# In the attention core, VectorE masks item w before it normalises item w-1

## What is computed

```
def attend_block(qb, keys, values, masks, sink):
    scale = HEAD_DIM ** -0.5
    ...
        s = jnp.einsum('bqkgd,bskd->bkgqs', qb, kp).astype(jnp.float32) * scale
        if mk is not None:
            s = jnp.where(mk, s, NEG_INF)
    ...
        m = jnp.maximum(m, jnp.max(s, axis=-1))
    denom = jnp.exp(sink_f - m)
    ...
        p = jnp.exp(s - m[..., None])
        denom = denom + jnp.sum(p, axis=-1)
        out = out + jnp.einsum('bkgqs,bskd->bqkgd', p.astype(vp.dtype), vp).astype(jnp.float32)
    out = out / jnp.moveaxis(denom, -1, 1)[..., None]
```

## Time and profile before

| | |
|---|---|
| time, median of 3 runs | 2988.97 us (2988.23 to 2990.68) |
| profiled execution, first to last instruction | 2988.2 us |
| profiled execution's own time | no more than 0.1 us from the fastest run, so nothing to speak of lies around the span |
| TensorE busy | 2801.6 us (94%) |
| VectorE busy | 1607.8 us (54%) |
| ScalarE busy | 1184.5 us (40%) |
| chain of work that ended last | TensorE 86%, VectorE 6%, ScalarE 6% |
| attention cores | 187.6 to 343.0 us and 2287 to 2442.7 us |

### The profile page before, as it was taken

How to read it: one execution, slowest core, us unless ns; L and a number is a source line. 1 busy time by engine, 2 the same in 40 slices (tenths; PEclk the granted TensorE clock), 3 DMA queues, 4 the chain that set the end, 5 groups by cost and what they waited for, 6 DMA issues and landing times.

```text
span 2988.2 us, 51513 instructions
## 1 busy us (share of the span) xinstructions
PE 2801.6 (94%) x19936; PEld 2645.5 (89%) x19936; DVE 1607.8 (54%) x2878; ACT 1184.5 (40%) x2042; POOL 109.7 (4%) x71
## 2 busy tenths in 40 slices
PE   5977799999998999999989999999998779999999
PEld 4965699999998999999969999999997569999999
DVE  2667556625644664366342665366367754663662
ACT  2347445414423552243232543244234754541441
POOL 1000010000002000000201000000100001000000
PEclk7989899999999999999989999999998989999999
DMA  6410133323320332333201332333121002221222
GB/s 233 181 64 1 50 125 134 137 74 135 136 93 33 138 134 103 123 133 130 66 24 57 120 134 100 111 134 127 63 78 36 1 15 61 78 84 64 73 85 74
DMA packets 62431, 279.67 MB, mean 94 GB/s; under 512 B 7392, under 2 KB 9568, under 8 KB 49632
## 3 DMA queue, kind: packets, MB, share of 16 engines
q1 hardware_dynamic: 62304, 277.93, 27.0%
HBM read 274.74 MB, written 3.16 MB: 93 GB/s over the span
## 4 chain that ended last, share of the span: by engine, by line
PE 86%; DVE 6%; ACT 6%; issue 2%; DMA 1%; SPq 0%; POOL 0%; DVEq 0%; ACTq 0%
PE ps L457 73%; ACT prob L923 3%; PE ps L541 3%; PE ps L480 3%; PE ps L743 1%; PE ps L552 1%; DVE prob L1265 1%; DVE prob L1282 1%; PE ps L502 1%; DMA ada_w<-in_ada_w 1%; ACT stat L925 1%; PE ps L680 1%; PE ps L649 1%; PE ps L510 1%; PE ps L635 1%
## 5 line engine op out<-in xcount | busy, mean ns | idle before, releaser
L457 PE MATMUL ps<-h_hi,w_hi 128*128 128x322 f32 x3392 | 799.8, 317 | 7.2 <-DVE w_lo L1057 4.1
L457 PE MATMUL ps<-h_lo,w_hi 128*128 128x322 f32 x3392 | 784.8, 313 | 0.0
L457 PE MATMUL ps<-h_hi,w_lo 128*128 128x322 f32 x3392 | 780.6, 312 | 0.0
L803 ACT ACTIVATE w_hi<-w_raw 128x1024 fp32r<-128x1024 f32 (+1 forms) x288 | 325.5, 1130 | 1037.1 <-PE ps L457 921.1
L457 PEld LDWEIGHTS ps<-h_hi,w_hi 128*128 128x128 f32 x3392 | 569.6, 190 | 34.0 <-issue 28.4
L457 PEld LDWEIGHTS ps<-h_lo,w_hi 128*128 128x128 f32 x3392 | 577.4, 190 | 0.0
L457 PEld LDWEIGHTS ps<-h_hi,w_lo 128*128 128x128 f32 x3392 | 577.0, 190 | 0.0
L1057 DVE TENSOR_TENSOR w_lo<-w_raw,w_hi 128x1024 fp32r<-128x1024 f32 (+1 forms) x288 | 377.3, 1310 | 67.6 <-ACT w_hi L803 65.9
L1177 DVE SCALAR_TENSOR_TENSOR x<-ps,mods,x 128x321 f32<-128x321 f32 (+5 forms) x264 | 99.9, 435 | 537.1 <-PE ps L457 537.1
L457 PE MATMUL ps<-f_hi,w_hi 128*128 128x322 f32 x1408 | 325.1, 312 | 0.0
L457 PE MATMUL ps<-f_hi,w_lo 128*128 128x322 f32 x1408 | 324.5, 312 | 0.0
(11 more groups left out here) (119 smaller groups left out, 2533.1 us busy)
## 6 DMA issues: line engine op xcount, KB each, us to landing
ada_w<-in_ada_w SPq DMA_DIRECT2D x96, 1024.0 KB, 5.5
w_raw<-in_w_in SPq DMA_DIRECT2D x176, 512.0 KB, 3.6
w_raw<-in_w_out SPq DMA_DIRECT2D x64, 704.0 KB, 4.0
w_raw<-in_w_qkv SPq DMA_DIRECT2D x24, 512.0 KB, 5.1
w_raw<-in_w_o SPq DMA_DIRECT2D x16, 512.0 KB, 3.8
w_raw<-in_w_fnet SPq DMA_DIRECT2D x8, 512.0 KB, 3.6
x<-in_x SPq DMA_DIRECT2D x1, 2576.0 KB, 15.5
out_y<-x SPq DMA_DIRECT2D x8, 322.0 KB, 3.7
```

Source lines behind the costliest of these rows:

```text
L457: mm = pe.matmul(ps[:, 2 * par + hf, 0:NH], w[par][:, kk, :], b[:, hf * NH:(hf + 1) * NH], start=(kk == 0 and n == 0), stop=(kk == k - 1 a ...
L803: act.activation(w_hi[par][:, 0:k, :], w_raw[par][:, 0:k, :], ACT.Copy).then_inc(hi_made, 1)
```

## The change

In VectorE's list `masked(w)` and `normed(w-1)` change places, in all 40 items of both attention layers. All functions, waits and semaphores stay as they are, and so do the lists of the other engines.

```diff
                     for w in range(w0, w0 + 43):
+                        if w < w0 + 40:
+                            masked(w)
                         if 1 <= w - w0 <= 40:
                             normed(w - 1)
-                        if w < w0 + 40:
-                            masked(w)
                         if w - w0 >= 3:
                             out_lo(w - 3)
```

## The result

| | before | changed |
|---|---|---|
| time, median | 2989.16 us (2988.23 to 2990.68) | 3052.47 us (3048.67 to 3055.38) |
| span of the profiled execution | 2988.2 us | 3053.6 us |
| VectorE busy, ScalarE busy | 1607.8, 1184.5 us | 1606.7, 1195.0 us |
| from the first L1279 to the last, first and second core | 146.0, 145.5 us | 175.2, 178.6 us |

Each time is the median of four runs. The profiled run of the changed kernel was the slowest of its four, 3055.38 us, so differences between profiles come out some 3 us larger than those between medians.

A forecast was written before the change was run, and what follows sets the result against it. A ring of waits through ScalarE was taken to bound both attention cores; the swap puts in TensorE's transposes and scores. 2988.2 + 2 x (20 ring + 17 clock) + 0.8 = 3063 us, chance 0.58; range 3020 to 3091.

The forecast's parts named there:

- What bounds the core: Both attention cores: no engine full; normalisation, masking and ScalarE's exponentials form a ring of waits, 4.10 us a turn.
- TensorE's leg: TensorE's transposes and the scores queued behind them, covered before the swap; 1.03 + 1.14 us in blocks 1 and 2.
- What enters the ring: In each core, masking now waits for transposes, then scores on TensorE; ScalarE's exponentials leave the ring.
- The turns: Time per item at full clock: 4.88 us in blocks 1 and 2, 4.44 in block 3, 4.10 in block 0.
- the hand-over from TensorE to VectorE: From the end of the scores to the masking, blocks 1 and 2: 0.05 us, bounds 0 and 0.1.
- The ring's sum: Longer turns over all blocks, clock as before: 20 us a core, 40 us for both.
- The clock: TensorE's clock falls in each core; a third of 31 turns at half level, 1.6 us each: 17 us a core.
- rival A: Both cores: the ring lengthens and the clock stays as before; 3029 us, chance 0.24.
- B: Rival: the clock stays at half level throughout the core, 50 us a core; 3129 us, chance 0.06.
- D: Rival: no change, as the leg is near 1.1 us or VectorE's steps keep the old rhythm; chance 0.06.
- C: Rival: the swap gains, exponentials hidden, VectorE's own 3.2 us an item is the ring; 2919 us, chance 0.06.

The follow-up runs named there:

- e4: Kernel before the change (normalisation first) with TensorE's scores one item further ahead; 2988.83 us.
- e10: Kernel before the change (normalisation first) with scores one item further ahead and a third pair of prob buffers; 2989.18 us.
- e12: Kernel before the change with TensorE doing the second head's transposes of each item twice; 2989.12 us.
- e1: Changed kernel with TensorE's list alone altered, scores one item further ahead; 2960.88 us.
- e3: Changed kernel with scores one item further ahead and a third pair of prob buffers; 2915.95 us.
- e2: Changed kernel with a third pair of prob buffers, TensorE's list as it was; 3049.21 us.
- e5: Changed kernel with TensorE computing each item's values twice into the same place; 3036.01 us.
- e7: Kernel before the change with each head's score matmuls issued twice; 3019.61 us.

## Why the prediction was right, step by step

- **What bounds the core** (a ring through ScalarE, TensorE's leg covered by 0.87 us): shown by e4, e10 and e12, in which TensorE's leg is shortened, freed or lengthened by 0.44 us in the old order and nothing moves.
- **What enters the ring** (transposes, then scores): shown by e1 to e3. Of the two waits the queue is the outer one, as e2 shows, and the buffer the next, as e1 shows.
- **The turns.** Forecast 4.88, 4.44 and 4.10 us, measured 4.95, 4.59 and 4.19. Four terms of block 1 are right within 0.01 (1.72, 0.94, 1.03, 1.14 against 1.72, 0.93, 1.02, 1.15). The mis-sized one is the hand-over from TensorE to VectorE: 0.05, taken from a hand-over to ScalarE, and outside its upper bound of 0.1; it is 0.13. The two engines do not hand over more slowly: in e1 VectorE's masking starts 0.04 behind TensorE (241.68 to 241.72), as ScalarE did, and its turn is 0.93 + 1.09 + 0.04 + 1.72 = 3.78 us. `masked(w)` waits for two semaphores. The masking instruction itself carries the wait for `t_done`, the last one in e1. The wait for `s_done`, the last one in the changed kernel, is an instruction of its own in VectorE's list (L1263; time lines leave such ones out). It starts at 259.06, some 0.03 behind the last matmul, and the masking follows at 259.16. So the term that was missing is some 0.1 us of VectorE's own, from that wait to the masking. In block 3 another 0.07 is in the transposes, 0.87 us until the scores for the 0.80 that the old trace had (291.19 to 291.99):

```profile
311.70 0.94 PE L635 MATMUL ps<-ident,prob 128*128 128x128 f32 x6 [1.66 <-DVE prob L1282]
...
312.57 0.71 PE L620 MATMUL ps<-qkv 64*128 64x256 f32 x4
```

There a head has three transposes of 0.11, and the second head's scaled rows come 0.40 behind the first's (0.88 for two L1282 of 0.48), so that TensorE waits between the heads; in the old order both were long ready. In block 4 at half level the spacing is 3.21 us, +0.55 for +0.46.
- **The ring's sum**, 40 us, is 45.4 with the clock nearly held (e5).
- **The clock** was expected to fall and rise several times in each core, and did. Its term is too large: 34 us for about 17. The number of turns was right: besides the first one, 8 of the first core's and 11 of the second's turns up to block 4 were longer than at the full level, a third as assumed. What was wrong is that I charged each with a whole turn at half level, 1.6 us, and most had the low clock for a part of it only, as the one at 276.68 with 0.78 us; the 19 together cost some 15 us, 0.8 each. One of the reasons for a fall was a misreading too: the new ring's idle stretches, 1.7 and 1.85 us, are not longer than all that held before. The old kernel kept its full level through one of 1.99 us:

```profile
318.84 0.66 PE L649 MATMUL ps<-probT,v_tok 128*64 128x128 f32 x8 [1.99 <-ACT probT L935]
```

So the length of its idle stretches gave no ground for the falls that were forecast, and in that they came by luck.
- **The Trainium skill** ("TensorE: Matmul & The Clock Gate", section "Why this matters for your kernels") names long idle gaps between bursts as what costs the clock mid-kernel. Taken as the only cause, they would have made it rival A. The changed kernel's TensorE was never idle for more than 1.84 us in blocks 1 to 3 at the full level, and lost its clock there several times. The measurement decides: in this loop shorter gaps were enough.
- **The rivals.** A (clock as before) is what e5 nearly makes by force; it gives 3036 us for the 3029 of A. B and D did not occur. C, the gain through hidden exponentials, was placed at 2919 us under the condition that TensorE's leg be under 1.09 us; e3 meets the condition by taking the leg out of the ring and gives 2915.95. The 1.85 us that the prediction gives this leg is 1.74 by its own terms (0.1 + 0.5 + 1.14); either is far above 1.09.

The two errors, 5 us too little for the ring and 17 too much for the clock, have opposite signs. That the forecast of 3063 comes as near to 3052 as it does is in part luck; the mechanism, TensorE's leg in the ring and its clock with it, is as forecast.

## What to carry to other kernels

Moving a step ahead on one engine moves its waits too: what stands behind them is now held by whatever feeds the step, and in a ring of three engines the leg that was covered can be longer than the one that was exposed. Before such a swap, add up the new ring from the old trace, from the released instruction through the other engine's queue back to the moved one, and compare it with the old ring; if it is longer, look first at what in the other queue can go ahead and which buffer forces the rest. Edits that each show nothing or a loss can be a gain together, so they are to be judged by the ring and not one by one.

## What the runs showed of the hardware

- TensorE's granted clock is part of a ring's price once TensorE is in it: with some half of its idle 1.76 us of each 4.95 filled by useless matmuls (e5), the kernel was 16 us faster. Before the fall behind 277 TensorE was busy 13.09 of 21.00 us at the full level; in the old kernel it held at 4.89 of 8.00. By busy share the two are alike, 0.62 and 0.61. What decides between them stays open.
- From TensorE's last matmul to the next engine's start it took 0.04 us, to ScalarE and to VectorE (e1) alike, where the waiting instruction carried the wait; where the wait was a separate instruction ahead of it (changed kernel, L1263), it took 0.13 us.
- Scores of two heads, on separate halves of the rows, ran at the same time where their passes stood next to each other in TensorE's list, 1.15 us for both (257.88 to 259.03); two passes of one head ran one behind the other. Issued as first, first, second, second (e7), the four passes took 2.90 us, three times the 0.97 of one (241.92 to 242.89), and not twice.
